# Last stage as all gates, then the output projection by pairs of tiles in seven block products for eight; first dilated key rows requested sooner

## What is computed

```python
def mixer_output(x, o_lat, o_b, o_c, gate, w_uv, w_out):
    B, S, _ = x.shape
    o_a = jnp.einsum('bshc,chd->bshd', o_lat, w_uv).reshape(B, S, MIX_A)
    o = jnp.concatenate([o_a, o_b.reshape(B, S, MIX_B), o_c.reshape(B, S, MIX_C)], axis=-1)
    return x + (o * jax.nn.silu(gate)) @ w_out
...
    idx = buf_len + np.arange(T)[:, None] - r * np.arange(n + 1)[None, :]
    valid = jnp.asarray(idx >= 0)
    kg = k_cat[:, idx]
```

## Time and profile before

| | us |
|---|---|
| runs | 1824.79, 1829.24, 1830.71 |
| median | 1829.24 |
| profiled execution | 1827.89 |
| its span in the trace, and what lies around it | 1826.2 and 1.7 |
| busy in the span: TensorE, VectorE, ScalarE, GpSimd | 1751.6 (96%), 1081.5 (59%), 809.0 (44%), 359.6 (20%) |
| last stage, from its first own gates to the span's end | 1457.5 to 1826.2 |

### The profile page before, as it was taken

One profiled execution on the slowest core, in us unless ns is written; L12 is line 12 of the kernel. 1 busy time (PEld: TensorE's weight loads), 2 busy tenths in 40 slices (PEclk: granted clock), 3 DMA queues, 4 the chain that ended last, 5 costly groups with the idle time before them and its releaser, 6 DMA issues. The chain is left out here.

```text
span 1826.2 us, 46660 instructions
## 1 busy us (share of the span) xinstructions
PE 1751.6 (96%) x18320; PEld 1354.2 (74%) x18320; DVE 1081.5 (59%) x2810; ACT 809.0 (44%) x1778; POOL 359.6 (20%) x505
## 2 busy tenths in 40 slices
PE   7999999998999989999999988999999899999998
PEld 6989898776778767777777755666666688888886
DVE  5434343587855567677776775677777843333332
ACT  5323232687952355566555622333333533333332
POOL 0101011255203040124210221211111431111110
PEclk9999999999999999999999998999999999999999
DMA  8764645643465731013110379999986744444441
GB/s 312 158 135 104 139 107 124 195 141 118 136 163 161 228 108 28 19 42 86 27 28 19 122 258 287 306 296 292 292 278 243 199 142 131 138 143 132 131 137 61
DMA packets 291276, 281.57 MB, mean 154 GB/s; under 512 B 138984, under 2 KB 255544, under 8 KB 286008
## 3 DMA queue, kind: packets, MB, share of 16 engines
q1 hardware_dynamic: 277576, 186.60, 39.0%
q0 software_dynamic: 13520, 92.43, 13.5%
HBM read 215.09 MB, written 55.48 MB: 148 GB/s over the span
## 5 line engine op out<-in xcount | busy, mean ns | idle before, releaser
L104 PE MATMUL proj_acc<-proj_w_hi,proj_x_hi 128*128 128x512 f32 (+2 forms) x512 | 182.5, 356 | 10.9 <-DVE proj_x_lo L362 9.0
L105 PE MATMUL proj_acc<-proj_w_lo,proj_x_hi 128*128 128x512 f32 (+2 forms) x512 | 182.0, 356 | 0.0
L106 PE MATMUL proj_acc<-proj_w_hi,proj_x_lo 128*128 128x512 f32 (+2 forms) x512 | 181.7, 355 | 0.0
L1874 DVE CUSTOM_DVE_ANT_0 mla_probs<-mla_scores,keep_in_rms 128x512 f32<-128x512 f32 x192 | 124.8, 687 | 56.6 <-PE mla_scores L1746 56.3
L1824 ACT ACTIVATE mla_probs<-mla_probs,mla_bias 128x256 f32<-128x256 f32 (+15 forms) x128 | 153.0, 1197 | 8.2 <-DVE mla_bias L1878 7.0
L1746 PE MATMUL mla_scores<-prompt_kr_parts,mla_q_parts 64*128 64x512 f32 (+3 forms) x640 | 134.3, 366 | 0.0
L104 PEld LDWEIGHTS proj_acc<-proj_w_hi,proj_x_hi 128*128 128x128 f32 x512 | 97.4, 190 | 22.1 <-issue 9.0
L2447 ACT ACTIVATE dec_probs<-dec_scores,sample_nb 128x1024 f32<-128x1024 f32 x32 | 35.7, 1114 | 158.7 <-DVE sample_nb L2528 158.7
L105 PEld LDWEIGHTS proj_acc<-proj_w_lo,proj_x_hi 128*128 128x128 f32 x512 | 97.5, 190 | 10.6
L106 PEld LDWEIGHTS proj_acc<-proj_w_hi,proj_x_lo 128*128 128x128 f32 x512 | 97.4, 190 | 10.4
L886 ACT ACTIVATE win_probs<-win_probs,win_rec 128x256 f32<-128x256 f32 (+1 forms) x192 | 86.6, 454 | 20.5 <-DVE win_rec L922 20.2
(11 more groups left out here) (466 smaller groups left out, 4455.2 us busy)
## 6 DMA issues: line engine op xcount, KB each, us to landing
featT<-proj_blocks SPq DMA_DIRECT2D x68, 180.0 KB, 4.9
win_v_tile<-wv_out SPq DMA_DIRECT2D x75, 128.0 KB
memory_x_raw<-in_xT SPq DMA_DIRECT2D x17, 512.0 KB, 5.5
proj_rows<-in_x SPq DMA_DIRECT2D x17, 512.0 KB, 3.7
host_buf<-in_xT SPq DMA_DIRECT2D x17, 512.0 KB, 6.7
late_ckv<-in_x SPq DMA_DIRECT2D x17, 512.0 KB, 3.8
y_out<-late_ckv POOLq DMA_DIRECT2D x16, 512.0 KB, 6.5
late_ckv<-late_ckv SPq DMA_DIRECT2D x248, 32.0 KB, 1.8
```

The costliest lines, as they stand in the source:

```text
L104: pe.matmul(out, lh, rh, start=start, stop=False)
L105: pe.matmul(out, lh, rl, start=False, stop=False)
L106: return pe.matmul(out, ll, rh, start=False, stop=stop)
L1874: dve.tensor_tensor_reduce(probs[:, u % 2, w, c * CH:c * CH + wide], scores[:, n % 3, 0:wide], add, -MLA_SCALE, -LOWEST, ALU.add, ALU.min, ...
```

## The change

In the window: the key rows of the first sequence are requested ahead of the wait for `pv_done` 3, which now stands between them and the memory keys. Item 4 moves on GpSimd's queue from before the memsets to behind them, and its gather waits for `pv_done` 2.

In the last stage: the order of tiles is 0 to 13, the sample tile, 14, 15. All gates come first. The gate's PSUM is double (two tiles), and so is x. Each gated tile, transposed by blocks on VectorE, is stored to a scratch tensor `mT` in DRAM (`store_blocks`, 16 DMAs of 32 KB, 8 for the sample tile) instead of moved in SBUF. w_out comes in four quarters of 512x512 rows by columns (`load_quarter`, four DMAs each, in the first four tiles), and sums of quarters are formed (`combine`). Seven of these parts are split, each 128x2048: four in the gates' phase, three after it.

Then come the sample tokens (`new_tokens`, 32 matmuls, high and low part side by side in 128 columns), and eight pairs of prompt tiles. A pair's two tiles and two halves of features make a 2x2 block matrix; w_out is another; their product is made of seven block products of 12 matmuls each, in place of eight. For this GpSimd makes four sums of blocks (`make_sums`) for the operands and adds four terms to the rows (`add_rows`); ScalarE and VectorE split seven operands; VectorE forms two middle sums (`middle_sums`) and adds five banks of PSUM (`add_bank`). Products rotate through eight banks. Outputs are stored from SP. The diff, cut:

```diff
@@ -2092,9 +2092,9 @@
             if s:
                 sp.wait_ge(win_turned, 8 * s)
                 sp.wait_ge(win_scored, 2 * s)
-            else:
+            load_rows(k_rows, "win_k", s, win_k_loaded)
+            if not s:
                 sp.wait_ge(pv_done, EARLY)
-            load_rows(k_rows, "win_k", s, win_k_loaded)
             sp.dma_start(mem_kT[:], io["mem_kT"][s].rearrange("(h p) m -> p h m", p=P)).then_inc(win_k_loaded, 16)
...
             pool.indirect_dma_start(kr[:, u, :], None, kr_rows, rows).then_inc(item_loaded[u], 16)
+            if before == 0:
+                pool.wait_ge(pv_done, 2)
             if before >= 1:
                 pool.wait_ge(pv_done, 2 * before + 2)
             pool.indirect_dma_start(items[u].rearrange("p m c -> p (m c)"), None, ckv_rows, rows).then_inc(item_loaded[u], 16)
 
-        for n in range(ITEMS_EARLY, ITEMS + 1):
+        for n in range(ITEMS_EARLY, ITEMS):
             load_item(n)
...
+    ORDER = [*range(14), LAST, 14, 15]
+    ring = [gate[:, i // 2, i % 2, :] for i in range(4)] + [prod[:, i, :] for i in range(4)]
+    bank_of = lambda p, i: ring[(7 * p + i) % 8]
...
+    W_FROM = {B11: Q11, B21: Q21, B22: Q22, T3: Q12, T1: Q11, T2: Q22, T4: Q21}
+    W_ORDER = [B11, B21, B22, T3, T2, T1, T4]
+    PRODUCTS = [B11, T3, T2, T1, B21, T4, B22]
...
+        return [pair_raw[:, 0, :, 0, :], sums[S3], sums[S2], sums[S1], pair_raw[:, 0, :, 1, :], pair_raw[:, 1, :, 1, :], sums[S4]][i]
+
+    SUMS_OF = [0, 2, 3, 1, 0, 0, 4]
...
+        def load_quarter(i):
+            c, d = divmod(i, 2)
+            if i == 0:
+                sp.wait_ge(late.w_low, 1)
+            sp.wait_ge(w_low, 2 * i + 1)
+            src = io["w_out"].rearrange("(q c j f) n -> c q f j n", q=4, c=2, f=UNIT)[c]
+            for q in range(4):
+                sp.dma_start(by_k(quarter[i])[UNIT * q:UNIT * q + UNIT, :, :], src[q][:, :, HALVES[d]]).then_inc(quarter_loaded[i], 16)
+
+        def store_blocks(t):
+            sp.wait_ge(blocks_turned, t + 1)
+            dst = turned_tokens(ORDER[t]).rearrange("(f i) (b x) -> f b i x", f=4, b=4)
+            for q in range(NS // UNIT if t == NEW_AT else 4):
+                for f in range(4):
+                    sp.dma_start(dst[f][q], block_rows[t % 2][UNIT * q:UNIT * q + UNIT, f * 256:(f + 1) * 256]).then_inc(blocks_stored[t % 2], 16)
+
+        def load_pair(p):
+            if p:
+                sp.wait_ge(op_low, 7 * p)
+                sp.wait_ge(sums_made, 4 * p)
             else:
...
+                sp.wait_ge(part_low, w_at[T3])
+            for t in (ORDER.index(2 * p), ORDER.index(2 * p + 1)):
+                sp.wait_ge(blocks_stored[t % 2], stored_until(t))
+            sp.dma_start(quarter[Q12].rearrange("p (i x) -> p i x", i=2),
+                         io["mT"][2 * p * P:(2 * p + 2) * P, :].rearrange("(i p) x -> p i x", p=P)).then_inc(raw_loaded, 16)
+
+        def load_rows(p):
...
+        for t in range(1, NT):
+            if t + 1 < NT:
+                sp.wait_ge(x_low, t)
+                load_x(sp, t + 1)
+            if t == NT - 1:
+                sp.wait_ge(blocks_stored[NEW_AT % 2], stored_until(NEW_AT))
+                sp.dma_start(new_raw.rearrange("p b c x -> p (b c x)"), turned_tokens(LAST)[:, 0:512]).then_inc(new_loaded, 16)
+                load_pair(0)
+            sp.wait_ge(gated_done, t)
+            load_mix(sp, t)
+            store_blocks(t - 1)
+            if t <= 4:
+                load_quarter(t - 1)
+            if t == 4:
+                sp.dma_start(f_gain[:], io["final_gain"].rearrange("(o n) -> o n", o=1).broadcast_to([P, D])).then_inc(consts, 16)
+        sp.wait_ge(gated_done, NT)
+        sp.dma_start(new_rows[NEW, :], io["x"][LAST * P:LAST * P + NS, :]).then_inc(new_rows_loaded, 16)
+        store_blocks(NT - 1)
+        load_rows(0)
+        load_pair(1)
+        load_rows(1)
+        sp.wait_ge(normed, 1)
+        sp.dma_start(io["y_out"][LAST * P:LAST * P + NS, :], new_rows[NEW, :]).then_inc(new_stored, 16)
+        for p in range(1, PAIRS):
+            if p + 1 < PAIRS:
+                load_pair(p + 1)
+                load_rows(p + 1)
+            store_tile(p - 1, 1, 2 * p).then_inc(rows_stored[(p - 1) % 3], 16)
+            store_tile(p - 1, 0, 2 * p + 1).then_inc(rows_stored[(p - 1) % 3], 16)
...
+        def make_sums(p):
+            pool.wait_ge(raw_loaded, 16 * (p + 1))
+            if p:
+                pool.wait_ge(op_low, 7 * p)
+            else:
+                pool.wait_ge(x_low, NT - 1)
+                pool.wait_ge(new_low, 3)
+            (a1, a2), (b1, b2) = ([pair_raw[:, i, :, c, :] for c in range(2)] for i in range(2))
+            pool.tensor_tensor(sums[S1], b1, b2, ALU.add).then_inc(sums_made, 1)
+            pool.tensor_tensor(sums[S3], b1, a1, ALU.subtract).then_inc(sums_made, 1)
+            pool.wait_ge(sums_made, 4 * p + 1)
+            pool.tensor_tensor(sums[S2], sums[S1], a1, ALU.subtract).then_inc(sums_made, 1)
+            pool.wait_ge(sums_made, 4 * p + 3)
+            pool.tensor_tensor(sums[S4], a2, sums[S2], ALU.subtract).then_inc(sums_made, 1)
+
+        def add_rows(p):
+            mine = rows[p % 3]
+            pool.wait_ge(rows_loaded[p % 3], 16 * (p // 3 + 1))
+            pool.wait_ge(bank_read, READS * p + 2)
+            for reads, i, cols, term in ((2, 1, HALVES[0], u3), (3, 1, HALVES[1], u3), (4, 0, HALVES[1], u2), (5, 0, HALVES[0], first_kept)):
+                if reads > 2:
+                    pool.wait_ge(bank_read, READS * p + reads)
+                pool.tensor_tensor(mine[:, i, cols], mine[:, i, cols], term, ALU.add).then_inc(rows_added, 1)
...
+        def gates(t):
+            for c in range(2):
+                act.wait_ge(gate_done, 2 * t + c + 1)
+                act.wait_ge(blocks_turned, t)
+                act.activation(gated[:, HALVES[c]], gate[:, t % 2, c, :], ACT.Silu, scale=in_rms[:, ORDER[t]:ORDER[t] + 1]).then_inc(silu_done, 1)
...
+        def operand(p, i):
+            if SUMS_OF[i]:
+                act.wait_ge(sums_made, 4 * p + SUMS_OF[i])
+            act.wait_ge(raw_loaded, 16 * (p + 1))
+            if p:
+                act.wait_ge(prod_done, 7 * (p - 1) + i + 1)
             else:
...
+                act.wait_ge(gate_done, 2 * NT)
+                if i == 6:
+                    act.wait_ge(new_done, 2)
+            act.activation(by_token_block(operands[i][0]), by_feature_block(source_of(i)), ACT.Copy).then_inc(op_high, 1)
...
+        early = {2: B11, 4: B21, 5: B22, 7: T3}
+        for t in range(NT):
+            gates(t)
+            if t + 2 < NT:
+                split_x(t + 2)
+            if t == NT - 2:
+                new_operands()
+            if t in early:
+                split_high(act, early[t])
...
+                for i in range(3, 7):
+                    operand(p + 1, i)
+                act.wait_ge(bank_read, READS * p + 7)
+                act.wait_ge(rows_added, ADDS * p + 4)
+                square(2 + 2 * p, rows[p % 3][:, 0, :])
+                keep_first(p + 1)
+                roots(1 + 2 * p)
+                roots(2 + 2 * p)
...
+        def middle_sums(p):
+            dve.wait_ge(kept_first, p + 1)
+            dve.wait_ge(prod_done, 7 * p + 3)
+            if p:
+                dve.wait_ge(rows_added, ADDS * p)
+            else:
+                dve.wait_ge(blocks_stored[0], stored_until(NT - 1))
+            dve.tensor_tensor(u2, first_kept, bank_of(p, 2), ALU.add).then_inc(bank_read, 1)
+            dve.wait_ge(bank_read, READS * p + 1)
+            dve.tensor_tensor(u3, u2, bank_of(p, 1), ALU.add).then_inc(bank_read, 1)
...
+            middle_sums(p)
+            if more:
+                operand(p + 1, 0)
+            dve.wait_ge(rows_loaded[p % 3], 16 * (p // 3 + 1))
+            add_bank(p, 3, 1, HALVES[1])
+            add_bank(p, 3, 0, HALVES[1])
+            add_bank(p, 4, 0, HALVES[0])
+            add_bank(p, 5, 1, HALVES[0], adds=1)
+            if more:
+                operand(p + 1, 1)
+                operand(p + 1, 2)
+            else:
+                means(j, j + 1)
+            add_bank(p, 6, 0, HALVES[1], adds=3)
+            if more:
+                for i in range(3, 7):
+                    operand(p + 1, i)
+                means(j, j + 1)
+                means(j + 1, j + 2)
+                scale(j, rows[p % 3][:, 1, :])
+                scale(j + 1, rows[p % 3][:, 0, :])
...
+        READ_BEFORE = [0, 0, 2, 1, 4, 5, 6]
+
+        def product(p, i):
+            w = PRODUCTS[i]
+            pe.wait_ge(op_low, 7 * p + i + 1)
+            if p == 0:
+                pe.wait_ge(part_low, w_at[w])
+                if i == 0:
+                    pe.wait_ge(silu_done, 2 * NT)
+                if i == 6:
+                    pe.wait_ge(new_whole, 4)
+            elif i == 0 and p >= 2:
+                pe.wait_ge(bank_read, READS * (p - 1))
+            elif i == 1:
+                pe.wait_ge(kept_first, p)
+            elif i > 1:
```

(54 more changed lines are left out.)

547 lines of the change are left out of this document (294 added, 253 removed).

## The result

The changed kernel takes 1.0063 of the time before, with a 95% interval of 1.0046 to 1.0081 over 11 runs of each: 1841.8 us in the median against 1830.7, or +11.5 us (8.4 to 14.8).

What follows compares the result with a forecast made beforehand. TensorE's matmuls were taken to bound the last stage. -27.0 (matmuls) + 10 (gates) + 17 (products) + 1.0 (tail) - 8.5 (window) = -7.5 on 1827.9 gave 1820.4, taken as a median of 1822 us; range 1806 to 1850.

Steps and rivals of the forecast that it cites:

- Matmuls taken away: Last stage on TensorE: 112 fewer matmuls, no turn of the first tile, no idle of 0.65; -27.0 us.
- The gates: Gates' phase of the last stage: SP's queue falls behind and GpSimd's merges are lengthened; +10 us.
- just even with 10.88: Gates: SP's issues per tile, with 0.15 of waits, sum to 10.85 us against TensorE's 10.88.
- The store's price: Gates, SP's queue: each 32 KB store from SBUF to DRAM has a pitch of 0.47 us.
- the rival that every store costs what a move does: Gates: stores have a pitch of 0.626, so the phase is +39 and the time 1851; chance 0.20.
- The products: Phase of the eight pairs: a loop of 20.8 us against TensorE's 19.04, and a late first pair; +17 us.
- a rival with a loop of 22.2: Products: each GpSimd add meets a two-input VectorE operation; loop 22.2 to 22.5, phase +26, time 1831; chance 0.10.
- The tail: After the last matmul: the other tile's scaling and an add of two sums of squares come first; +1.0 us.
- The window: First ride of the sample window: key rows requested 5.9 us sooner, item 4 slightly late; -8.5 us.
- the ride's 10.1 us: Window: the first ride's 15.93 us against an ordinary 5.83, taken as the most that can be had.
- The rival "pays nothing": Window: item 4 is late by the key rows' gain, or the next wait takes over; 1831; chance 0.10.
- the slower side's chance: Whole kernel: slower than 1834.7 us, from dearer stores and far ends of two other rivals; chance 0.28.

Runs made afterwards that it cites:

- e3: Changed kernel with each tile's blocks stored by 4 DMAs of 128 KB for 16 of 32 KB: 0.9926 of the time before, -13.5 us.
- e5: Changed kernel with eight of a tile's sixteen stores issued from ScalarE's queue: 0.9990 of the time before, -1.8 us.
- e6: Changed kernel without the scaling of two of three window patterns in the merge, sixteen stores kept: 1.0009 of the time before.
- e4: Changed kernel with GpSimd making the next pair's sums before adding this pair's rows: 1.0020 of the time before.
- e1: Kernel before with the window edit alone (first key rows requested ahead of the wait, item 4 behind the memsets): 0.9983 of the time before, -3.1 us.
- e2: Changed kernel with the window edit undone, so the last stage's change alone: 1.0086 of the time before, +15.7 us.
- e10: Changed kernel with four stores a tile and the next pair's sums first, window edit undone: 0.9898 of the time before, -18.7 us.
- e8: Changed kernel with four stores a tile and the next pair's sums ahead of the row adds: 0.9880 of the time before, -22.0 us.
- e7: Kernel before with its first key rows requested ahead of the wait, item 4 left where it was: 1.0001 of the time before.
- e9: Kernel before with the window edit and item 6's gather of values cut from 2 MB to 256 KB: 0.9947 of the time before, -9.7 us.

## Why the prediction was wrong, point by point

**Matmuls taken away: right.** -27.0 forecast, 361.2 less 333.7 = -27.5 measured.

**The gates: wrong, +10 forecast and +22.4 measured.** This is the step that failed. What was wrong is "just even with 10.88": the sum of SP's issues, with 0.15 of waits in it, was taken as the tile's time. But SP's list has a wait in it, for the gated tile, whose mix SP itself requested one turn before. In the trace that wait comes to 10.4 us in the gates, and this ring was never added up. From rows of the kernel before it is a request (1.9 to the shares' issue), a landing of 1.9, a merge of 3.4 and a product of 1.24: 8.4 us undisturbed, with little margin to 10.88. In the trace it is 11.8 and 12.9 in the two tiles shown, where x (512 KB) goes directly ahead of the mix, whose shares then land after 4.55 in the longer one, and where the merge takes 5.4 and 5.7. It is 16.5 where a quarter of w_out stands ahead too.

The store's price was nearly right. It is 0.46 for 0.47 where nothing disturbs the queue, and the rival that every store costs what a move does (0.626) is out. But the mean pitch is 0.50, since single issues took up to 1.79 (median 0.42), and 0.50 is where the forecast itself put the turn to a loss. That is 0.4 a tile, at most 6 of the 12 us missed, and less where SP would have waited anyway; why these issues are longer stays open. The four quarters and f_gain took SP 7.8 us, as forecast (8).

Tiles 2 to 5, counted from 0, into which the quarters' loads fall, cost 13.1 of the 22.4 (1474.04 to 1530.69, less 4 x 10.88), of which 3.6 are the clock (below). The eleven behind them, for which the forecast had 2 at most, cost 9.3. e3 and e5 show that SP's issues hold the ring: fewer of them leave 0.9 and 3.4 of the 22.4. e6 shows the merge's part, 5.3.

**The products: right in mechanism, +17 forecast and +15.0 measured.** The loop was put at 20.8; the trace has 20.05 between the idles of 1777.57 and 1797.62, near the sum without a lengthened operation, 20.1, though some were lengthened (below), so that other terms must be smaller. GpSimd's 128x512 was taken at 1.3; here are its operations in the kernel after:

```profile
L2948 POOL TENSOR_TENSOR late_ckv<-late_ckv,fin_blocks 128x512 f32<-128x512 f32 x24 | 30.7, 1297 | 85.8 <-DVE fin_blocks L3153 76.4 <-DVE late_ckv L3160 9.4
L2939 POOL TENSOR_TENSOR host_buf<-late_ckv,host_buf 128x512 f32<-128x512 f32 x8 | 13.1, 1632 | 0.6
```

The loop's excess counted in four pairs (3.2 us) for six (11), most likely since the first pair's waits gave the others a lead; and those waits were larger, 7.9 for 5 to 6, with 1.8 more for the clock behind them and some 2 of longer steps elsewhere. That 15.0 is near 17 is in part luck: the terms missed to both sides. e4 shows that GpSimd's work is in the loop.

**The rule on the shared port.** In merge after merge GpSimd's scalings are lengthened where VectorE works beside them: the first takes 2.63 beside a VectorE operation on two inputs from 1578.79 to 1581.07, and 0.91, where 0.60 is its own time; a pair takes 3.23 for 1.18, beside a VectorE operation that itself took 2.70 for 2.28. The Trainium skill's page "SBUF — State Buffer", section "SBUF: two separate sides", has this as an exclusive lock held for a whole instruction; these rows agree. In the products the rule was a rival with a loop of 22.2. It didn't come to that: most row adds and sums took 1.30. The last sum of a pair was lengthened (a mean of 1.63), one more a little (1.43), and three of VectorE's low parts (0.88, 1.10 and 1.56 for 0.68), and the loop was 20.05. In the gates the forecast gave it 2 us. There the scalings of 15 merges took 50.0 us, where 0.605 each would be 27.2; e6, which leaves out two of three, says that they are worth 5.3 in time.

**The tail: right**, +1.0 forecast, +0.9 measured.

**The window: wrong, -8.5 forecast and -3 to -4 measured** in three comparisons (e1, e2 beside the changed kernel, e10 beside e8). The second failed step is the bound of it: the ride's 10.1 us were read as a wait for a request that came late, and the share of the DMA engines was not read in the same stretch. It was full, 1.13 in 1097 to 1104. An earlier request then mostly changes who is late: the wait went to the value rows in the traces of e1, e7 and the kernel after, and in e5 and e6 the time was lost behind the ride. e9's time fits this. Where the 3 to 4 us come from stays open. The 4 us from 1080 on in which the engines stood at 0.41 are not enough of a reason, since e7 fills them (1.16) and gains nothing. The rival "pays nothing" came nearer, at a chance of 0.10.

**The sum.** -27.5 + 22.4 + 15.0 + 0.9 - 3.3 = +7.5; measured +11.5 (8.4 to 14.8). The 4.0 (1 to 7) between them stay open. By e2 the last stage's change is +15.7 (11.0 to 20.5), where its trace has 10.9 in that stage; of the rest, the sample items are 3.5 longer before the fifth in that trace, under unchanged code. In the range, 1806 to 1850, the time did lie; the sign was wrong, and the slower side's chance, 0.28, was carried by a rival (the store's price) that was at most a part of the cause.

## What to carry to other kernels

Where a stage is split so that an engine works a tile off in half the time, every ring of a tile has to be added up against the new step, not only each engine's or queue's load: a queue whose instructions wait for something it has itself requested has a length beyond its busy time. In these runs a queue paid for the number of DMAs and hardly for their size, so count them first: gathering the same pieces into four for sixteen was worth 25 us. And before a wait for a DMA is priced as gain, read the share of the DMA engines in the same stretch: at a share of 1.13 a wait of 7.79 us gave 3 to 4. A wait of that kind differs by several us from one execution to the next, so take its price from many runs and not from one trace.

## What the runs showed of the hardware

The granted clock fell after some short idles and not after others. Windows of the kernel after, the clock in the third column from the end, behind idles of 2.73, 3.88, 1.84, 2.69 and 5.65 us:

```profile
1488.00:1492.00 4.00, 4.00 (x13) 3.11 (x13) 0.88 (x1) 0.00 (x0) 2.83 (x5) 0.66 0.37 100
1516.00:1520.00 4.00, 3.95 (x10) 3.13 (x11) 0.63 (x1) 0.00 (x0) 3.08 (x5) 0.57 0.37 75
1530.00:1536.00 6.00, 5.31 (x23) 4.43 (x24) 3.25 (x2) 2.34 (x3) 5.79 (x5) 1.00 0.48 135
1555.00:1561.00 6.00, 5.56 (x24) 4.62 (x25) 3.19 (x3) 0.28 (x1) 5.52 (x5) 1.00 0.27 71
1697.00:1701.00 4.00, 3.97 (x10) 3.17 (x11) 3.88 (x5) 4.00 (x8) 1.13 (x1) 0.51 0.00 0
```

Where it fell, it went to its lower level of 1.2 GHz for some of the window. Behind the idle of 2.73 the next 24 gate matmuls took 7.2 us for 5.44, so that this idle cost 4.5. After idles of 2.69 and 1.84 nothing of the kind was seen. What tells the cases apart wasn't tried.

A DMA of SBUF to DRAM with 128 pieces of 1 KB was issued in 0.44 in the median (e3), one with 32 such pieces in 0.42 (the kernel after); they landed 2.9 and 1.8 us later.
